# A feed-forward stage rebuilt: block products for the up projection, the down projection as a phase of its own

## The reference, cut to what matters

```python
def feed_forward(x, pre, post, w_up, conv_w, conv_b, w_down):   # shortened
    h = rms_norm_2(x, pre)
    u = causal_dwconv(h @ w_up, conv_w) + conv_b     # 1024 -> 2 x 2816, three taps over tokens
    gate, value = split(u, 2)
    y = (silu(gate) * value) @ w_down                # 2816 -> 1024
    return x + rms_norm_2(y, post)
```

## Time and profile before

| what | us |
|---|---|
| median of 3 runs | 2539.48 (2538.57 to 2539.82) |
| the profiled execution, device time | 2536.68 |
| its span, first to last instruction | 2535.0 |
| PE busy in it | 2407.4 (95%) |
| DVE, ACT, POOL busy | 1188.5, 1011.8, 626.9 |

### The profile page before, as it was taken

The page is one execution under the profiler, slowest core; times in us unless marked ns, Lnnn a source line. Parts: engine busy times, 40 slices in busy tenths (PEclk is TensorE's granted clock), DMA queues, the critical chain, the costliest instruction groups (busy, mean ns, idle before and its releaser), DMA issues. The chain is left out here.

```text
span 2535.0 us, 32879 instructions
## 1 busy us (share of the span) xinstructions
PE 2407.4 (95%) x13084; PEld 1963.1 (77%) x13084; DVE 1188.5 (47%) x1650; ACT 1011.8 (40%) x2123; POOL 626.9 (25%) x291
## 2 busy tenths in 40 slices
PE   6989999889999999899999998989999999999997
PEld 4777787678887777677888886668788888888886
DVE  5845303784653502685550465641644343333336
ACT  4434323674533433474534354653522121212123
POOL 2211120232321121132321130112334242423331
PEclk9999999899999999899999998999999999999999
DMA  6432110104202110003211100013111111121213
GB/s 240 138 111 75 34 50 1 34 1 158 75 25 92 43 55 29 17 18 117 83 50 42 40 1 9 22 37 134 59 50 50 50 50 50 34 67 34 67 47 144
DMA packets 130862, 154.54 MB, mean 61 GB/s; under 512 B 7309, under 2 KB 100884, under 8 KB 130710
## 3 DMA queue, kind: packets, MB, share of 16 engines
q1 hardware_dynamic: 129669, 152.44, 17.8%
q10 hardware_dynamic: 1040, 0.00, 0.0%
HBM read 135.65 MB, written 16.78 MB: 60 GB/s over the span
## 5 line engine op out<-in xcount | busy, mean ns | idle before, releaser
L812 PE MATMUL ps<-hT_hi,w_hi 128*128 128x512 f32 x1064 | 415.3, 390 | 4.3 <-PEq L272 2.8
L812 PE MATMUL ps<-hT_hi,w_lo 128*128 128x512 f32 x1064 | 414.7, 390 | 0.0
L812 PE MATMUL ps<-hT_lo,w_hi 128*128 128x512 f32 x1064 | 414.5, 390 | 0.0
L812 PEld LDWEIGHTS ps<-hT_hi,w_hi 128*128 128x128 f32 x1064 | 200.1, 188 | 46.3 <-issue 4.9
L812 PEld LDWEIGHTS ps<-hT_lo,w_hi 128*128 128x128 f32 x1064 | 200.2, 188 | 41.5
L812 PEld LDWEIGHTS ps<-hT_hi,w_lo 128*128 128x128 f32 x1064 | 200.0, 188 | 41.6
L748 POOL TENSOR_TENSOR w_lo<-ffn_raw,w_hi 128x2048 fp32r<-128x2048 f32 (+1 forms) x32 | 163.1, 5097 | 109.0 <-ACT w_hi L722 109.0
L3843 DVE TENSOR_SCALAR work<-work,fcols 128x1024 f32<-128x1024 f32 x44 | 33.3, 756 | 284.7 <-ACT work L3800 284.7
L3800 ACT ACTIVATE work<-ps 128x512 f32<-128x512 f32 x88 | 52.5, 598 | 277.8 <-PE ps L812 275.3
L722 ACT ACTIVATE w_hi<-ffn_raw 128x2048 fp32r<-128x2048 f32 (+1 forms) x32 | 59.6, 1864 | 236.4 <-PE ps L812 149.1
L3824 POOL TENSOR_TENSOR ffn_hid_lo<-work,ffn_hid_hi 128x1024 fp32r<-128x1024 f32 x22 | 65.0, 2956 | 336.0 <-ACT ffn_hid_hi L3814 336.0
(11 more groups left out here) (502 smaller groups left out, 5361.3 us busy)
## 6 DMA issues: line engine op xcount, KB each, us to landing
ffn_raw<-in_ffn_w_up SPq DMA_DIRECT2D x40, 512.0 KB, 4.7
mix_gla<-in_w_ada SPq DMA_DIRECT2D x32, 512.0 KB, 3.6
xres<-big SPq DMA_DIRECT2D x24, 512.0 KB, 2.6
difp_raw<-in_w_in SPq DMA_DIRECT2D x10, 1024.0 KB, 5.0
ffn_raw<-in_ffn_w_down SPq DMA_DIRECT2D x10, 1024.0 KB, 5.0
...
```

The source lines that it names most:

```text
L812: mm = nc.tensor.matmul(out, l, r, start=(job.part != 1 and c == 0 and k == 0), stop=(job.evac and c == job.chunks - 1 and k == 2))
```

## The change

`stage_ffn` and `last_rows` are replaced. `UpOperands` and `DownOperands` name the tiles. The stage no longer uses `stage_project`.

- **Plain part.** Up jobs 0, 1 and 2 are computed as before (12 units, through 6 PSUM banks; job 2's weights go through the old slot).
- **Block products.** For the other 19 jobs the product is seen as 2x2 blocks: gate or value columns, first or second 4 chunks, first or second 512 tokens. Seven products of 12 matmuls replace eight, in Winograd's form. Four sums of token blocks (`t1` to `t4`, 128x2048 each) are made once, by eight DVE operations, and split by ACT and POOL while the plain part runs. Four sums of weight blocks (128x512) are made by DVE for every job. Every weight operand is split in 128x512 pieces (7 by ACT, 7 by POOL a job), in 8 slots.
- **Putting together.** Products 0 to 2 start three PSUM banks; products 3 to 6 are added into the same banks after ACT or DVE has read the sum so far. DVE makes the four output halves with five 128x512 operations, ACT with two copies. The value's taps are written to PSUM (banks 6, 7), the gate's to SBUF (`sg`). `u` and the taps' outputs have one buffer each.
- **Features** go to a DRAM tensor `hid` (22 stores of 512 KB) and come back in halves of 512 tokens.
- **Down phase.** 44 steps: 22 chunks for tokens 0 to 511, then the 22 in reverse order for the rest. A step is 4 token tiles by 2 column halves by 3 matmuls into 8 PSUM banks, so `y` is never in SBUF. The first 3 and the last 6 chunks of each half go tile by tile. 14 weight rows stay for the second half, 8 are loaded again. Norm and store of a tile follow its last matmul.

In the diff below `FIRST` and `LAST` are 3 and 6. In round s (job s + 3), products 0, 1 and 2 wait until the bank's last reader of round s-2 (`c11`, `c21`, `c12`) is done. `q1` waits for product 0 and for the value's taps of the job before; `high` of a weight sum waits for all four sums of its job; `conv(j, ...)` is three taps; `store(j)` waits for feature j.

The diff, cut:

```diff
+WINOGRAD = (("a11", "b11", 0), ("s2", "t2", 1), ("s1", "t1", 2), ("s3", "t3", 1), ("a12", "b21", 0), ("a22", "t4", 1),
+            ("s4", "b22", 2))
...
+    def steps(self):
+        f, l = self.FIRST, self.LAST
+        for a in (0, NF):
+            yield list(range(a, a + f)), (2, 0, 1, 3) if a == 0 else (0, 1, 2, 3), False
+            for k in range(a + f, a + NF - l):
+                yield [k], (0, 1, 2, 3), False
+            yield list(range(a + NF - l, a + NF)), (0, 1, 2, 3), True
...
+        cv = m.ps[:, 6:8, :].rearrange("p b n -> p (b n)")
...
         def _(sp):
+            for j in range(PLAIN, NF - 1):
+                store(j - 1)
+                if j + 3 < NF:
+                    load(j + 3)
...
         def _(pool):
+            opening.staging_free(pool)
+            part(0, 0, quarter(1))
+            part(1, 2, quarter(0))
+            part(2, 1, quarter(2))
+            pool.wait_ge(s_hi, 1)
+            b = std_half(2)
+            pool.tensor_tensor(m.w_lo[:, b, :], raw[:, 0, :], m.w_hi[:, b, :].bitcast(F32),
+                               ALU.subtract).then_inc(s_lo, 1)
+            part(3, 3, quarter(1))
+            for n in range(ALLPROD):
+                low(n)
...
         def _(pe):
+            def winograd(s):
...
+                pe.wait_ge(s_q2, s + 1)
+                product(NPROD * s + 3)
+                pe.wait_ge(s_q1, s + 1)
+                product(NPROD * s + 4)
+                pe.wait_ge(s_e, s + 1)
+                product(NPROD * s + 5)
+                pe.wait_ge(s_c22, s + 1)
+                product(NPROD * s + 6)
...
         def _(act):
+            opening.settled(act)
+            empty(0)
+            part(0, 0, quarter(1), 3)
+            empty(1)
+            part(1, 2, quarter(0), 5)
+            empty(2)
+            part(2, 1, quarter(2), 6)
+            empty(3)
+            act.wait_ge(s_raw[0], 32)
+            act.wait_ge(s_std, 4)
+            nc.scalar.activation(m.w_hi[:, std_half(2), :], raw[:, 0, :], ACT.Copy).then_inc(s_hi, 1)
+            silu(0)
+            empty(4)
+            part(3, 3, quarter(1), 8)
+            empty(5)
+            empty(6)
+            silu(1)
+            empty(7)
+            empty(8)
+            for n in range(4):
+                high(n)
+            for g in range(9, 12):
+                empty(g)
+            for n in range(4, 8):
+                high(n)
+            for s in range(NWINO):
...
+                q1(s)
+                silu(s + PLAIN - 1)
+                if s < NWINO - 1:
+                    for n in range(NPROD * s + 8, NPROD * s + 12):
+                        high(n)
+                    c11(s)
+                    for n in range(NPROD * s + 12, NPROD * s + 15):
+                        high(n)
...
         def _(dve):
+            tsum(a, *region(0, 1), ALU.add, 0)
+            tsum(b, *region(0, 0), ALU.add, 0)
+            tsum(b, a, b, ALU.subtract, 2)
+            tsum(c, *region(1, 1), ALU.add, 0)
+            tsum(a, c, a, ALU.subtract, 4)
+            tsum(c, c, b, ALU.subtract, 5)
+            dve.wait_ge(s_pad, 1)
+            plain_conv(0, 0)
+            plain_conv(0, 1)
+            dve.wait_ge(s_tlo, 1)
+            tsum(b, *region(1, 0), ALU.add, 6)
+            feature(0)
+            dve.wait_ge(s_tsum, 7)
+            tsum(b, b, c, ALU.subtract, 0)
+            plain_conv(1, 0)
+            plain_conv(1, 1)
+            feature(1)
+            weight_sums(0)
+            plain_conv(2, 0)
+            plain_conv(2, 1)
+            for s in range(NWINO):
+                j = s + PLAIN
+                dve.wait_ge(s_prod, NPROD * s + 2)
...
+                add(u_half(0, 1), u_half(1, 0), s, 1, s_q2)
+                feature(j - 1)
+                if s + 1 < NWINO:
+                    weight_sums(s + 1)
+                dve.wait_ge(s_prod, NPROD * s + 4)
+                add(u_half(1, 1), u_half(1, 0), s, 1, s_e)
+                dve.wait_ge(s_e, s + 1)
+                add(u_half(1, 1), u_half(1, 1), s, 2, s_c22)
+                dve.wait_ge(s_prod, NPROD * s + 6)
+                add(u_half(1, 0), u_half(1, 0), s, 1, s_c21)
...
+                conv(j, 1, cv)
+                dve.wait_ge(s_prod, NPROD * s + 7)
+                add(u_half(0, 1), u_half(0, 1), s, 2, s_c12)
...
+                conv(j, 0, sg[:, :])
```

More of the change, by code:

```diff
@@ L3614, in stage_out_plain @@
         return opening
[L3618 to L3733, removed]
@@ L3738, in ffn_up_job @@
                spread=(j == 0))
-def stage_ffn(nc, m, w_up, w_down, y, fcols, work, w_post, out, xres, base, block, opening):
-    GROUP, RING = 4, 5
-    pad = FFN_K - 1
[L3748 to L3784, removed]
@@ new lines, in stage_ffn @@
+def stage_ffn(nc, m, w_up, w_down, hid, fcols, w_post, out, xres, block, opening):
+    pad = FFN_K - 1
+    with ExitStack() as ctx:
+        (s_ev, s_std, s_prod, s_hi, s_lo, s_tsum, s_thi, s_tlo, s_sum, s_pad, s_tap, s_conv, s_silu, s_f, s_st,
+         s_q1, s_c11, s_q2, s_e, s_c22, s_c21, s_c12) = semaphores(
+            nc, ctx, m, "ffn", "ev std prod hi lo tsum thi tlo sum pad tap conv silu f st q1 c11 q2 e c22 c21 c12")
+        s_raw = semaphores(nc, ctx, m, "ffn", "raw0 raw1")
+        s_hraw, s_wraw = (semaphores(nc, ctx, m, "down", " ".join(f"{n}{b}" for b in range(DownOperands.STAGED)))
+                          for n in ("hraw", "wraw"))
+        s_x, s_out = (semaphores(nc, ctx, m, "postf", " ".join(f"{n}{b}" for b in range(3))) for n in ("x", "out"))
+        (s_hhi, s_hlo, s_whi, s_wlo, s_wlov, s_step, s_fin, s_act, s_r, s_t, s_new, s_w) = semaphores(
+            nc, ctx, m, "down", "hhi hlo whi wlo wlov step fin act r t new w")
@@ L3785, in sb @@
         def sb(name, shape, dt=F32):
             return ctx.enter_context(m.tensor("ffn_" + name, shape, dt))
[L3788 to L3807, removed]
-            nc.scalar.activation(q.sg, q.cv[:, 0, :], ACT.Silu, bias=bias(j, 0)).then_inc(q.extra["silu"], 1)
@@ L3868, in pe_job @@
-    def pe_job(pe, q, t, job):
-        if job.tag[0] == "down" and job.tag[2] == 0 and not job.hold:
-            pe.wait_ge(q.extra["hlo"], groups[job.tag[1]][-1] + 1)
-    def tail(ctx, block, q):
-        slots = [(m.w_hi[:, (len(jobs) - 2 + k + base) % 2, :], m.w_lo[:, (len(jobs) - 2 + k + base) % 2, :])
-                 for k in range(2)]
+        ssq, bias, r = sb("ssq", [P, 2, NT]), sb("bias", [P, NT]), sb("r", [P, NT])
+        raw, sums = sb("raw", [P, 2, KC * WCOLS]), sb("sums", [P, 2, 4, 512])
@@ new lines, in stage_ffn, with tap, u_half, std_half @@
+        rows = [u[:, 0, 0:D], u[:, 1, 0:D], f[:, :]]
+        def tap(j, k, up):
+            c = 2 * NF * k + NF * up + j
+            return fcols[:, c:c + 1]
+        def u_half(up, half):
+            return u[:, up, pad + 512 * half:pad + 512 * half + 512]
+        def std_half(t):
+            return (t + 1) % 2
+        def conv_done(j, up):
+            first = 1 if j >= PLAIN else 0
+            return 2 * j + (1 if up == first else 2)
+        def bank(s, k):
+            return 3 * (s % 2) + k
@@ L4052 @@
     a["xres"] = nc.dram_tensor("xres", (S, D), F32, kind="Internal").ap()
+    a["hid"] = nc.dram_tensor("hid", (FFN, S), F32, kind="Internal").ap()
     a["out"] = nc.dram_tensor("out", (1, S, D), F32, kind="ExternalOutput").ap()
```

540 lines of the change are left out of this document (467 added, 73 removed).

## The result

| | us, median (lowest to highest) |
|---|---|
| kernel before | 2539.65 (2538.57 to 2541.56), 4 runs |
| kernel after | 2505.59 (2505.21 to 2506.28), 4 runs |
| ratio | 0.9864, 95% interval 0.9851 to 0.9876 |

The change takes 34 us off, 1.36%. The forecast was 2504 with 35 us. The profiled execution took 2506.28 with a span of 2504.5, where the one of before had 2536.68 and 2535.0.

The account below looks back on a forecast made before the run. The prediction took PE's count of matmuls to bound the body, with a row-by-row epilogue behind. Unstalled span 2477.5 plus 19.0 opening, 2 clock, 1 last round gave 2499.5; plus 1.7 and 2.8 made 2504 us, range 2482 to 2530.

Parts of the forecast that it names:

- PE's count: Feed-forward stage: seven products for eight remove 228 matmuls at 0.2268 us each, worth 51.7 us.
- The end: Behind the last matmul: only the last tile's epilogue is bare, 7.1 us where 13.1 stood before.
- The rounds at PE's pace: The 19 block-product rounds: 19.05 us each, zero added, `q2` 1.2 us to spare, up to 1 us each as far end.
- the second rival: Rounds up to 1 us late in each of 19, or steps 0.5 in 44: 2508 to 2530 us, chance 0.20.
- The opening: Stage start to round 1: DVE and POOL take turns, PE stalls 4.9, 3.2, 4.8 and 6.1 us, sum 19.0.
- the walk: Instruction-by-instruction timing of the opening from 1814.38, giving PE's four stalls, 19.0 us in sum.
- Clock: PE at the 1.2 GHz level after opening stalls, counting only behind the last: between 0 and 6 us, 2 taken.
- The last round: Last block-product round: POOL's first four feature splits meet the gate's taps, making `q2` 1 us late.
- The down phase: The 44 down-projection steps, 5.44 us each: other engines hidden, between 0 and 0.5 us lost a step, 0 taken.
- The sum: Whole kernel: 2477.5 + 19.0 + 2 + 1 = 2499.5 us of span, 2504 as median.
- the hiding opening: Rival for the opening: POOL's large splits slip between DVE's sums, stalls 0 to 6, 2482 to 2488 us, chance 0.15.
- the slower rival: Rounds: POOL's splits delay DVE's SBUF instructions, DVE sets the round, 3.8 x 19 = 72 us more, 2576, chance 0.10.

Follow-up runs that it names:

- e7: The kernel after with product 0 of every round computed twice, 228 matmuls more: 2551.28 us, ratio 1.0052 to the kernel before.
- e8: The kernel after with only the last chunk of each token half done tile by tile, not the last six: 2507.23 us, ratio 0.9877.
- e5: The kernel after with the value's first tap done twice in each of the 19 rounds: 2513.68 us, ratio 0.9896.
- e6: The kernel after with the value's first tap done three times in each round: 2538.44 us, ratio 0.9998.
- e4: The kernel after with two token lows and job 2's low weights on DVE, two lows moved on POOL, a sum and an emptying earlier: 2480.43 us.
- e2: The kernel after with POOL writing zeros instead of subtracting for the four token lows, part of the computation left out: 2482.95 us, ratio 0.9780.

## Why the prediction was right

By its own steps:

- **PE's count.** Held: 228 fewer, 0.2267 us each, 51.7 (e7: +51.7 before what it hid).
- **The end.** Held: 7.1 forecast and 7.1 from the last matmul's end (7.5 from its start), and bare for one tile alone (e8).
- **The rounds at PE's pace.** Held: 19.04 forecast as 19.05. The value's scaling into PSUM took 1.29 (1.23 was taken), and `q2` had 1.06 to spare (1.2 was forecast). e5 and e6 show that this small margin was all that stood between the forecast and the second rival.
- **The opening.** Held, in mechanism and in size: `q2` was to let product 3 of round 0 start 81.5 us into the stage and did so at 80.8, a loss of 18.2 for 19.0. The waits are at the four places named and in their order, but only two have the size of the walk: 4.60 (4.9 forecast) before unit 8, 0.98 (3.2) before product 0, 4.74 (4.8) before product 1, 3.36 (6.1) before product 3, together 13.7. The other 4.3 before product 3 were lost at the lower level (1.6 behind unit 8, 2.7 behind product 1): PE came later to products 0 and 3 and waited less there. Besides, the operands of products 0 and 3 were each 0.7 earlier than in the walk.
- **Clock.** Held: 1.7 for 2. All in all 6.0 were lost at the lower level, but the walk's term is for what lies behind the last of the four waits. e7 bears out that what PE does ahead of it costs nothing as long as `q2` is the later: there, 12 more matmuls ahead of product 3 moved its start by 0.07.
- **The last round.** Held: 0.86 for 1. The gate's taps there took 0.82, 2.21 and 2.20 for 0.75 and twice 1.28.
- **The down phase.** Held at zero: 1056 matmuls in one piece.
- **The sum.** The stage was to take 2499.5 - 1814.4 = 685.1 and took 683.8, so the steps together were off by 1.3. The span was 5 us over its forecast of 2499.5 because the stretch before the stage took 6.3 longer in this execution, which the sum took as fixed and which isn't of the change. The median of after was 0.7 below its profiled time, where before lay 2.8 above; these two, 5.0 too long and 3.5 too short, nearly cancel by luck: 2505.59 against 2504 is closer than the forecast of the span was.

Of the rivals, the hiding opening is what e4 makes of the kernel (2480.43, where 2482 to 2488 was worked out for it), but not as the rival had it, by sums slipping between splits at less cost. A 2048-wide sum took its 2.28, and it still waited out a split; in e4 the large splits were taken away from where DVE reads SBUF, among other edits. Late rounds came with e5. DVE's instructions slowed by POOL in every round, the slower rival, did not occur: with the sums and taps of a round where they are, the period stayed at PE's pace, and in the round shown the gate's taps kept 0.75, 1.29 and 1.28.

Open is how much of e2's gain is the memset's shorter time, how e4's edits share its gain, and why the granted clock before the stage differs between executions.
